# Layer-1 modulation units of the grouped attention: one per item, or two in every even item

## The reference, cut to what matters

```python
for layer in range(DEPTH):
    mod_l = jnp.split((s_lat @ ada_w[layer] + ada_b[layer])[:, None, :], 6, axis=-1)
    mod_c = jnp.split((s_ctx @ ada_w[layer] + ada_b[layer])[:, None, :], 6, axis=-1)
    ...
def attend_gqa(q, keys, vals):
    s = jnp.einsum('bqhgd,bkhd->bhgqk', q, keys).astype(F32)
    p = jax.nn.softmax(s, axis=-1).astype(vals.dtype)
    return jnp.einsum('bhgqk,bkhd->bqhgd', p, vals)
```

## Time and profile before

| what | value |
|---|---|
| median of three runs | 2619.45 us (2611.97, 2619.45, 2626.12) |
| profiled execution, its span | 2621.1 us |
| PE busy in it | 2159.6 us, 82% |
| DVE, ACT, POOL busy | 698.7, 462.1, 169.9 us |
| mean granted TensorE clock | 0.917 of full speed |
| grouped attention stage, from the span's start | 234 to 416 us |

### The profile page before, as it was taken

How to read it: one execution, slowest core, us unless ns; L and a number is a source line. 1 busy time by engine, 2 the same in 40 slices (tenths; PEclk the granted TensorE clock), 3 DMA queues, 4 the chain that set the end, 5 groups by cost and what they waited for, 6 DMA issues and landing times.

```text
span 2621.1 us, 31425 instructions
## 1 busy us (share of the span) xinstructions
PE 2159.6 (82%) x13016; PEld 1113.8 (42%) x13016; DVE 698.7 (27%) x1289; ACT 462.1 (18%) x1025; POOL 169.9 (6%) x156
## 2 busy tenths in 40 slices
PE   5998999963686949999999968998999487777774
PEld 0643666643686423333333324544895222222221
DVE  1106332268857151111001112000552500000001
ACT  1113221167521011000000012000551100000001
POOL 0000000011111000111111010000000000000000
PEclk8998999975768979999999989999999699999997
DMA  8225432023202337999999961102212399999996
GB/s 335 85 96 192 143 115 70 9 74 98 73 18 107 134 143 298 390 392 392 388 388 386 384 235 49 56 25 84 69 41 90 128 400 415 415 414 415 414 415 237
DMA packets 113955, 564.30 MB, mean 215 GB/s; under 512 B 13552, under 2 KB 26352, under 8 KB 64672
## 3 DMA queue, kind: packets, MB, share of 16 engines
q1 hardware_dynamic: 102080, 522.55, 51.1%
q0 software_dynamic: 10416, 34.58, 4.8%
q10 hardware_dynamic: 1328, 5.24, 0.5%
HBM read 532.87 MB, written 29.46 MB: 215 GB/s over the span
## 4 chain that ended last, share of the span: by engine, by line
PE 63%; DMA 22%; DVE 9%; ACT 2%; issue 2%; SPq 1%; POOL 0%; DVEq 0%; ACTq 0%; POOLq 0%
PE ps L1805 14%; DMA work_sb<-expert_w_up 7%; PE ps L1569 5%; PE ps L1813 5%; DMA work_sb<-expert_w_gate 5%; DMA work_sb<-expert_w_down 5%; PE ps L458 4%; PE ps L2071 4%; PE ps L754 3%; PE ps L643 2%; PE ps L2049 2%; PE ps L2058 2%; PE ps L241 2%; PE ps L2134 2%; DMA ring_sb<-expert_w_up 2%
## 5 line engine op out<-in xcount | busy, mean ns | idle before, releaser
L1805 PE MATMUL ps<-work_sb 128*32 128x512 f32 (+1 forms) x2304 | 364.9, 600 | 74.2 <-DMA work_sb<-expert_w_gate 32.7
L1805 PE MATMUL ps<-ring_sb,work_sb 128*32 128x512 f32 (+1 forms) x2304 | 365.0, 605 | 66.5 <-DMA ring_sb<-expert_w_up 31.0
L1805 PEld LDWEIGHTS ps<-work_sb 128*32 128x32 f32 (+1 forms) x2304 | 114.5, 120 | 306.9 <-issue 306.5
L1805 PEld LDWEIGHTS ps<-ring_sb,work_sb 128*32 128x32 f32 (+1 forms) x2304 | 109.4, 121 | 293.7 <-issue 275.9
L1913 DVE TENSOR_TENSOR work_sb<-ps,work_sb 128x512 f32<-128x512 f32 x32 | 20.6, 687 | 663.3 <-PE ps L1813 334.1
L1569 PE MATMUL ps<-ring_sb,work_sb 128*128 128x512 f32 x320 | 139.6, 599 | 2.7 <-DVE work_sb L2199 1.9
L1884 ACT ACTIVATE work_sb<-ps 128x1024 f32<-128x1024 f32 x16 | 16.4, 1023 | 605.9 <-PE ps L1805 305.9
L241 PE MATMUL ps<-ring_sb,sT_sb 128*32 128x512 f32 x384 | 99.5, 677 | 25.3 <-DMA ring_sb<-ada_w 25.2
L1964 POOL DMA_INDIRECT hl_rows<-work_sb x32 | 45.6, 1425 | 971.3 <-DVE work_sb L1927 872.0
L458 PE MATMUL ps<-ring_sb,work_sb 128*128 128x512 f32 (+1 forms) x288 | 105.9, 530 | 0.9 <-DVE work_sb L353 0.9
L1813 PE MATMUL ps<-ring_sb,work_sb 128*32 128x512 f32 x768 | 101.4, 598 | 0.0
(11 more groups left out here) (363 smaller groups left out, 2796.3 us busy)
## 6 DMA issues: line engine op xcount, KB each, us to landing
work_sb<-expert_w_gate SPq DMA_DIRECT2D x64, 1024.0 KB, 10.0
ring_sb<-expert_w_gate SPq DMA_DIRECT2D x64, 1024.0 KB, 11.2
ring_sb<-expert_w_up SPq DMA_DIRECT2D x64, 1024.0 KB, 16.1
work_sb<-expert_w_up SPq DMA_DIRECT2D x64, 1024.0 KB, 14.0
ring_sb<-expert_w_down SPq DMA_DIRECT2D x64, 1024.0 KB, 13.6
work_sb<-expert_w_down SPq DMA_DIRECT2D x64, 1024.0 KB, 12.7
ring_sb<-ada_w SPq DMA_DIRECT2D x96, 512.0 KB, 5.7
ring_sb<-wout SPq DMA_DIRECT2D x16, 512.0 KB, 7.6
```

Of the source, the lines that this page charges most:

```text
L1805: mm = pe.matmul(ps[g:g + wide, bank + n, :], lat_src[:, k, g:g + wide], us[e][:, n * 512:(n + 1) * 512], start=(k == 0), stop=(k == KT - 1))
```

## The change

In the attention's item loop PE no longer does unit n in item n. In every even item n it first waits until units n and n + 1 have both landed, and then does both; odd items have no unit. Items, units and instructions are as many as before.

```diff
                 if n == 0:
                     pe.wait_ge(g_act, 1)
                     pe.wait_ge(g_rowT, 1)
-                ada_matmuls(pe, 1, n, 7)
+                if n % 2 == 0:
+                    landed(pe, ada_at(1, n))
+                    landed(pe, ada_at(1, n + 1))
+                    ada_matmuls(pe, 1, n, 7)
+                    ada_matmuls(pe, 1, n + 1, 7)
                 if n >= 1:
                     values(n - 1)
```

## The result

| | before | changed |
|---|---|---|
| median of four runs | 2617.27 us (2611.97 to 2626.12) | 2596.01 us (2585.68 to 2597.23) |
| span of the profiled execution | 2621.1 us | 2594.8 us |
| PE busy in it | 2159.6 us | 2138.9 us |
| convolution starts at | 415.91 us | 391.64 us |

The ratio of the changed kernel to the one before is 0.9902, with a 95% interval of 0.9877 to 0.9927, that is 19 to 32 us less. The kernel became faster, by about what was forecast (2594.7 us forecast, 2596.01 measured). The closeness of the two times is partly luck: the medians are 21.3 us apart where 24.8 was forecast, the median of before came out 2.2 us lower than the one that the forecast started from, and runs of one kernel differ by 12 to 14 us. The terms are therefore tested on the attention stage in the traces, where the difference is 24.4 us.

A forecast was written before the change was run, and what follows sets the result against it. The attention stage was taken as bound by PE's instruction stream; 19.2 + 5.6 + 0.7 - 0.5 - 0.2 = 24.8 us off a median of 2619.45 gave 2594.7 us, range 2586 to 2608 us.

The forecast's parts named there:

- The pair: Attention's even items: the second unit fills idle array columns and is nearly free, 0.02 us a pair.
- The row of layer 0: Trace of layer 0's units: two pairs went through in 1.92 us, read as 0.96 us for a pair.
- Odd long items: Sixteen odd items, 17 to 47, lose their unit: 1.2 us each, 19.2 us in all (15.7 to 19.4).
- the boundaries of a unit: Transposes before a unit and values behind it run longer: 0.09 + 0.14 = 0.23 us more gained without it.
- Odd short items: Eight odd items lose their unit: 0.8 us each for seven of them, 5.6 us.
- the chain: Short odd items: the next transposes wait for ACT's copy, so an item falls to about 1.44 us and not lower.
- Item 15: Last short odd item, followed by a long item with longer maximum and exponential: gains 0.7 us.
- the fuller pairs: All 24 pairs: second units cost 0.02 us each, 0.5 us lost in all.
- The new landing waits: PE wants unit n + 1 one item earlier; waits costed at nothing, 15 us of lead against 4.3.
- Through to the end: End of the attention stage: later work hangs on PE's stream, so the gain should pass through to the end.
- The two rivals that rested on this stage: Mixed clock between 545 and 800 us: gain lost later, 2607 to 2619 us, 6%; slower, up to 2642 us, 3%.
- The rival of a falling clock in the short items: Short section runs at 1.2 GHz, 19 us lost, long items' gain eaten: 2619 us; 3%.

The follow-up runs named there:

- the same groups: Changed kernel, but the second unit of each pair writes column groups 0 and 1 like the first, added on top; 2612.08 us, ratio 0.9978.
- the units apart: Changed kernel with the values product of the item before moved between the two units of the pair; 2620.05 us, ratio 1.0015.
- the dense kernel: Against the kernel before: a pair in each of the sixteen short items and in even items 16 to 30, none later; 2589.46 us, ratio 0.9917.
- the kernel with thinned units: Changed kernel with 16 instead of 512 moving columns in each matmul of layer 1's units; 2573.37 us in a single execution.

## Why the prediction was right

Step by step, with its sum of 24.8 us against 24.4 in the stage of the profiled execution:

- **The pair**: 0.02 us each forecast, 0.01 to 0.02 measured (0.99 to 1.00 against 0.98 us; odd units left out: 0.01). The row of layer 0 carried over, though it was read with a small slip: its 1.92 us is the length of overlapping records to the end of the last, while 0.98 is from start to start. Read in the same way, a single pair in the attention is 1.06 us long, so the second pair there added 0.86 us. The runs with the same groups and with the units apart show both of its conditions: other groups, and next to each other.
- **Odd long items**: 1.2 us forecast, 1.18 measured from transposes to transposes, 1.16 in the kernel with long pairs only (18.6 us against 19.2). The choice near the upper bound was right, because the boundaries of a unit are real: 0.10 us before and, of the 0.14 forecast behind, 0.09 to 0.10 us, with weight loads that do not run ahead there. On the drain of TensorE at a change of tiling mode, which the Trainium skill states in TensorEngine Tiling (Array Packing), Key Properties, without a size, these traces agree with some 0.1 us at either side.
- **Odd short items**: 1.48 us forecast by the value taken (the chain alone gave 1.44), 1.48 measured. PE waits for ACT's copy as the chain said, though the wait is booked to the exponential. Item 15 gave 0.7 us as forecast; all eight together 5.7 us, forecast 5.6 + 0.7 less 0.2 and the fuller pairs, 5.9. The rest lies in the even items, which took 2.32 us where 2.28 and a pair's 0.02 were counted.
- **The new landing waits**: forecast at nothing, and none shows. The rate in short items, forecast 264 GB/s, was 260. But one number of this step was wrong: from 218 GB/s at a DMA share of 0.72 I had concluded that about 300 was possible. The changed kernel moves 260 at a share of 0.80, and the dense kernel 411 at 1.03. The share does not grow in proportion to the rate, so a limit read from it is too low. The kernel before's own trace could have said so: shortly before the stage, between 200 and 237 us, transfers that were nearly all of the same units ran at 394 to 421 GB/s for some 9 us. The step's result stood because the error was on the safe side.
- **Through to the end**: the convolution starts 24.3 us earlier and the span ends 26.3 us earlier. From the convolution's start to the end it was 2205.2 us before and 2203.2 after; over nine traces, those of the experiments included, it lay between 2192.8 and 2208.4 us with no relation to the change in the attention. The part between convolution and output projection lasted 296.8 to 307.4 us there. Its rows in the kernel before, the changed kernel, the one without odd units and the one with long pairs only:

```profile
545.00:848.60 303.60, 184.50 (x2229) 175.47 (x2227) 234.38 (x401) 137.22 (x335) 49.53 (x50) 0.67 0.23 78
```

```profile
520.40:826.70 306.30, 187.16 (x2231) 178.04 (x2229) 234.62 (x401) 137.59 (x336) 49.64 (x50) 0.66 0.24 77
```

```profile
519.70:816.50 296.80, 179.78 (x2230) 171.23 (x2228) 235.26 (x401) 137.46 (x336) 50.98 (x50) 0.68 0.24 79
```

```profile
522.40:829.80 307.40, 191.33 (x2230) 181.86 (x2228) 233.66 (x401) 137.65 (x336) 50.61 (x50) 0.66 0.23 77
```

PE's busy time moves with the granted clock (0.66 to 0.68) for the same work, while DVE's and ACT's stay: the shortest and the longest are 10.6 us apart, and their PE busy times 11.6. What sets that clock, and whether it is also what makes the runs of one kernel differ by 12 to 14 us, was not tested. The forecast's level has a small slip: a run's time is 1.8 us more than its span (2596.6 and 2594.8 us in the changed kernel), so the profiled execution of before lay by that some 3.4 us above its median and not 1.65; the 24.8 us do not depend on it. The two rivals that rested on this stage did not come about, but the spread is real and of the size of half the gain, which is why the range had to be wide.

The rival of a falling clock in the short items did not come about either: 1.00 in the changed kernel, and 1.00 between 246 and 267 us in the dense one. Nor did it show in the kernel with thinned units, whose short items took 1.5 us, even and odd, at 1.00.

## What to carry to other kernels

Matmuls of 32 stationary columns that fill half of the column groups cost here the same as those that fill all of them (0.98 and 1.00 us), if the other half's work stands right behind them on PE's list; look for a place in the same trace where they already do so, and take the price from there. Count with a unit also the 0.1 us at either side of a change between narrow and full-width matmuls. Where PE is the bound with little to spare, work out the chain through the other engines before counting the full gain: in short items it took a third of the possible 1.18 us.

## What was new about the hardware

- Two units of two matmuls each, in four column groups, took 1.00 us, and in two column groups 1.84 us, in one and the same order of instructions; with six full-width matmuls of 64 columns between them (twelve records) 0.98 us each.
- The weight loads of the matmuls behind a change between 32 and 128 stationary columns began with their first matmul, and without such a change 0.11 us ahead of it; each change cost 0.1 us.
- A DMA share of 0.72 stood beside 218 GB/s, 0.80 beside 260, and 1.03 beside 411 GB/s, all for transfers of 512 KB to the same ring; the median landing time was 4.3, 4.2 and 8.2 us.
- A pair of units with 16 moving columns still took 0.38 us of PE, half of it in its boundaries.
